# Start addresses of the weight rings in SBUF: from multiples of 2048 to 448 modulo 512

## The reference

```
def first_block(x, mem, ...):
    x = x + 0.5 * swiglu(rms_norm(x, norm_ffn1_w), ffn1_w_in, ffn1_w_out)      # d_ff 2816
    x = x + hybrid_mixer(rms_norm(x, norm_mix_w), w_in_mix, ...)               # SSD scan | differential attention
    x = x + memory_cross_attention(rms_norm(x, ..), rms_norm(mem, ..), w_cq, w_ck, w_cv, w_co)
    x = x + 0.5 * swiglu(rms_norm(x, norm_ffn2_w), ffn2_w_in, ffn2_w_out)
    return rms_norm(x, norm_final_w)

def second_block(x, p, ...):
    q, k, v, cb, cc, cu, ga, gc = split(rms_norm_2(x, g_pre_mix) @ w_in)
    o = stick_breaking_attention(q, k, v)
    y_conv = (cb * causal_depthwise_conv(cc * cu, w_conv)) @ w_conv_out
    x = x + rms_norm_2((gate_attn * (o @ w_attn_out) + gate_conv * y_conv) @ w_o, g_post_mix)
    x = x + rms_norm_2(square(relu(rms_norm_2(x, g_pre_mlp) @ w_up)) @ w_down, g_post_mlp)
    x = x + sigmoid(rms_norm_2(x, g_ple) @ w_ple_gate) * (p @ w_ple_proj)
```

## Time and profile before

| what | value |
|---|---|
| median of 3 runs | 2135.91 us (2134.52 to 2137.22) |
| span of the profiled execution | 2133.4 us |
| PE busy | 2114.8 us, 99% of the span, 10122 matmuls |
| POOL, DVE, ACT busy | 1120.5, 829.8, 803.6 us |
| granted TensorE clock | 1.00 |
| transfers | 207.71 MB, mean 97 GB/s |

### The profile page before, as it was taken

One profiled execution on the slowest core, in us unless ns is written; L12 is line 12 of the kernel. 1 busy time (PEld: TensorE's weight loads), 2 busy tenths in 40 slices (PEclk: granted clock), 3 DMA queues, 4 the chain that ended last, 5 costly groups with the idle time before them and its releaser, 6 DMA issues.

```text
span 2133.4 us, 29164 instructions
## 1 busy us (share of the span) xinstructions
PE 2114.8 (99%) x10122; PEld 1740.7 (82%) x10122; DVE 829.8 (39%) x1489; ACT 803.6 (38%) x1345; POOL 1120.5 (53%) x1493
## 2 busy tenths in 40 slices
PE   9999999999999999999999999999999999999999
PEld 7888888878887778877888888887787888888887
DVE  5222211762841766143322222208744474023244
ACT  5222232325834655323322223326554343122233
POOL 6555555673354337725655555554545466555554
PEclk9999999999999999999999999999999999999999
DMA  6322233233322213412332223321222223332322
GB/s 214 119 98 98 99 106 106 85 99 96 114 99 79 75 55 122 155 40 89 99 98 98 95 94 117 99 96 63 79 89 79 89 80 108 99 99 99 99 89 80
DMA packets 61344, 207.71 MB, mean 97 GB/s; under 512 B 6616, under 2 KB 8088, under 8 KB 61256
## 3 DMA queue, kind: packets, MB, share of 16 engines
q1 hardware_dynamic: 55216, 195.84, 27.8%
q10 hardware_dynamic: 6040, 10.65, 1.5%
HBM read 204.31 MB, written 4.77 MB: 98 GB/s over the span
## 4 chain that ended last, share of the span: by engine, by line
PE 42%; issue 28%; POOL 27%; DVE 2%; POOLq 0%; ACT 0%; DMA 0%; SPq 0%; DVEq 0%; ACTq 0%
POOL w_lo L463 27%; PE bank L516 11%; PE bank L518 11%; PE bank L517 11%; PE bank L678 1%; PE bank L680 1%; PE bank L679 1%; PE bank L908 1%; PE bank L932 1%; PE bank L840 1%; PE bank L920 0%; DVE gx_lo L2394 0%; DVE bank L2403 0%; PE bank L846 0%; DVE x L2405 0%
## 5 line engine op out<-in xcount | busy, mean ns | idle before, releaser
L463 POOL TENSOR_TENSOR w_lo<-w_raw,w_hi 128x256 fp32r<-128x256 f32 x1448 | 1087.1, 783 | 933.4 <-ACT w_hi L1283 933.3
L516 PE MATMUL bank<-gx_hi,w_hi 128*128 128x512 f32 (+1 forms) x1768 | 674.9, 382 | 7.8 <-DVE gx_lo L2394 4.5
L518 PE MATMUL bank<-gx_hi,w_lo 128*128 128x512 f32 (+1 forms) x1768 | 668.1, 378 | 0.0
L517 PE MATMUL bank<-gx_lo,w_hi 128*128 128x512 f32 (+1 forms) x1768 | 667.6, 378 | 0.0
L1283 ACT CAST w_hi<-w_raw 128x1024 fp32r<-128x1024 f32 x364 | 378.4, 1045 | 347.9 <-PE bank L518 291.8
L516 PEld LDWEIGHTS bank<-gx_hi,w_hi 128*128 128x128 f32 x1768 | 332.6, 188 | 74.2 <-DVE gx_lo L2394 6.4
L518 PEld LDWEIGHTS bank<-gx_hi,w_lo 128*128 128x128 f32 x1768 | 332.5, 188 | 62.1
L517 PEld LDWEIGHTS bank<-gx_lo,w_hi 128*128 128x128 f32 x1768 | 332.7, 188 | 60.5 <-issue 0.2
L516 PE MATMUL bank<-ff_hi,w_hi 128*128 128x512 f32 x352 | 136.9, 389 | 0.0
L517 PE MATMUL bank<-ff_lo,w_hi 128*128 128x512 f32 x352 | 136.9, 389 | 0.0
L518 PE MATMUL bank<-ff_hi,w_lo 128*128 128x512 f32 x352 | 136.9, 389 | 0.0
(11 more groups left out here) (358 smaller groups left out, 2703.4 us busy)
## 6 DMA issues: line engine op xcount, KB each, us to landing
w_raw<-wstream SPq DMA_DIRECT2D x364, 512.0 KB, 3.5
bias_spread<-bias_rows ACTq DMA_DIRECT2D x1, 2560.0 KB
square<-cum_rows ACTq DMA_DIRECT2D x8, 256.0 KB, 3.5
rfin_row<-cum_rows ACTq DMA_DIRECT2D x8, 256.0 KB, 3.1
outT<-ple_o SPq DMA_DIRECT2D x8, 256.0 KB, 2.0
x<-xT SPq DMA_DIRECT2D x3, 512.0 KB, 8.0
square<-bias_spread ACTq DMA_DIRECT2D x4, 256.0 KB, 2.6
rfin_row<-bias_spread ACTq DMA_DIRECT2D x4, 256.0 KB, 2.7
```

The lines of the kernel that those rows point to most:

```text
L463: ins = nc.gpsimd.tensor_tensor(w_lo[:, s, part], w_raw[:, s, part], w_hi[:, s, part].bitcast(F32), ALU.subtract)
L516: nc.tensor.matmul(dst, hi, rhs[0], start=first, stop=False)
L517: nc.tensor.matmul(dst, hi, rhs[1], start=False, stop=False)
L518: return nc.tensor.matmul(dst, lo, rhs[0], start=False, stop=last)
```

## The change

Ahead of the rings the cursor moves on by 448 bytes, and the order of the three is now `w_hi`, `w_lo`, `w_raw`. All three are 16 KiB long, so each begins at 448 modulo 512, and so does every block of 128 weights in them. `flip`, which nothing reads, is dropped from `consts` with its 128 columns; the slices of `consts` behind it shift by one. What lies from `rows` to `xrec` starts 64 bytes lower than before. REGION is at the same address as before, and with it every activation in it; `x`, `cols`, `wdt` and `gx` are ahead of the inserted bytes and stay as well. No engine's instructions are changed in kind, number, shape or order.

```diff
@@ -34,6 +34,7 @@
 LINE = 2048
+STATIONARY = 64
 RING = 4
@@ -162,10 +163,11 @@
         gx_hi = fixed("gx_hi", [DC, S], F32R)
         gx_lo = fixed("gx_lo", [DC, S], F32R)
-        w_raw = fixed("w_raw", [RING, UNIT])
+        cursor[0] += 512 - STATIONARY
         w_hi = fixed("w_hi", [RING, UNIT], F32R)
         w_lo = fixed("w_lo", [RING, UNIT], F32R)
-        consts = fixed("consts", [7 * P])
+        w_raw = fixed("w_raw", [RING, UNIT])
+        consts = fixed("consts", [6 * P])
         rows = fixed("rows", [NROWS])
@@ -195,7 +197,7 @@
-        ident, tri_le, ones, flip, neg_ge, neg_ones, tri_lt = (consts[:, i * P:(i + 1) * P] for i in range(7))
+        ident, tri_le, ones, neg_ge, neg_ones, tri_lt = (consts[:, i * P:(i + 1) * P] for i in range(6))
@@ -1610,7 +1612,7 @@
-            nc.scalar.copy(stick_r[:, 0:2, :], consts[:, 4 * P:6 * P].rearrange("p (a b) -> p a b", a=2))\
+            nc.scalar.copy(stick_r[:, 0:2, :], consts[:, 3 * P:5 * P].rearrange("p (a b) -> p a b", a=2))\
@@ -2543,7 +2545,7 @@
-    m = [np.eye(P, dtype=f), (i[:, None] <= i[None, :]).astype(f), np.ones((P, P), f), np.eye(P, dtype=f)[::-1],
+    m = [np.eye(P, dtype=f), (i[:, None] <= i[None, :]).astype(f), np.ones((P, P), f),
```

## The result

The kernel after takes 2151.47 us (median of 4 runs, 2150.16 to 2152.01) where the kernel before takes 2135.22 beside it: the ratio is 1.0075 with a 95% interval of 1.0061 to 1.0089. It is slower by 0.75%, where I had forecast 1.4% faster. The time is inside the stated range, but on its slow side, which I had given to the rivals, and outside the forecast's own range of 2086 to 2125 us.

A forecast was written before the change was run, and what follows sets the result against it. PE was taken as the bound, matmul count times pitch (start-to-start distance, 226.6 ns at 512 columns). Terms −31.9, −1.6 and +3.2 us net −30.3, off the median 2135.91: 2106 us, with 2078 to 2186 for 8 in 10.

The forecast's parts named there:

- The first term: 7344 matmuls of 512 columns with ring slices stationary: 4.35 ns less each, −31.9 us, ends −15.4 and −48.5.
- Ring slices as stationary, 512 columns: The step behind the first term: middle of 2.1 and 6.6 ns taken as gain on each of 7344 matmuls.
- the pitch of 220 to 224.5 ns: Sign that the forecast is right: start distance of 512-column matmuls in a window such as 1100 to 1122 us.
- 64 above costs, 64 below gains: Reading of two stages: stationary 64 bytes above moving costs 6.6 ns (`cv`), 64 below gains 2.1 ns (`ck`).
- Halves: 768 matmuls of 256 columns, `gx` and `up` in halves: 2.1 ns less each, −1.6 us.
- Token stages: 480 matmuls of `z`, `v`, `v2`, activations stationary and ring moving: 6.6 ns more each, +3.2 us.
- ACT, POOL, the transfers and the small tensors: Ring readers and writers off PE, and small tensors moved by 64 bytes: zero, being covered by PE's work.
- `ck` and `cv` at 128 apart: 192 and 96 matmuls whose operands come to 128 bytes apart: taken as 0, bounds ±0.4 and ±0.6 us.
- Rival 1: Plain 512-column matmuls lose a rhythm that needs equal starts: about +4.7 ns each, 2171 us; chance 0.22.
- Rival 2: Any stationary off a multiple of 512 costs what `cv` costs: +6.6 ns on 7344 matmuls, 2187 us; chance 0.14.
- Rival 3: Nothing happens: the pitch doesn't depend on where the ring stands, 2136 us; chance 0.10.
- Rival 4: Remainder beyond the columns goes almost entirely in the plain form: −11.6 ns on 7344 matmuls, 2052 us; chance 0.08.

The follow-up runs named there:

- rings0: Changed kernel with the three rings back on a multiple of 512, the 448 bytes behind them; 2135.49 us, ratio 1.0000 to the kernel before.
- all448: Changed kernel with `gx` and REGION also at 448 modulo 512, so operands start alike again; 2135.52 us, ratio 1.0003 to the kernel before.
- lo448: Changed kernel with `w_hi` on a multiple of 512 again, only `w_lo` and `w_raw` at 448; 2162.87 us, ratio 1.0127 to the kernel before.
- rings64: Changed kernel with its rings at 64 modulo 512 instead of 448; 2176.14 us, ratio 1.0190 to the kernel before.
- halves64: Changed kernel with rings at 0 modulo 256 and only the 16 units of 256-column matmuls 64 bytes higher; 2134.74 us, ratio 0.9999 to the kernel before.

## Why the prediction was wrong

**The first term had the wrong sign.** The step that failed is "Ring slices as stationary, 512 columns": I took −4.35 ns, the middle between 2.1 ns "of the right sign but half the columns" and 6.6 ns "of the right columns but the other sign". The sign came from `ck` at 256 columns, the size from `cv` at 512. Measured, the plain form went from 226.7 to 228.9 ns at its settled places, and on average over all its pitches without a pause from 227.05 to 229.08: a loss of 2.0 ns and not a gain of 4.35. In the trace the term is +14.4 us, where I had put −31.9. Of the signs named ahead, the pitch of 220 to 224.5 ns failed; the halves near 117.8, the token stages near 233 and the unchanged waits and engines all came.

**Why the sign did not carry over.** "64 above costs, 64 below gains" is wrong twice. At 512 columns the table has no gain on either side of 0: all distances cost but 16. At 256 columns the lowest pitch, 113.3, stands at +64, the side that "costs". What `ck` had over the earlier trace rows was not a gain of its distance over a neutral 0; at 256 columns 0 is a poor place, with 120.0. Equal starts are the best place for the one length and a poor one for the other, so a row of the one says nothing of the sign of the other. A pitch with all columns counted (213.3) was never near: the lowest at 512 columns in any trace was 226.7.

**The small terms held.** Halves: −1.6 us forecast, −0.9 in the trace, with 120.0 to 117.8 ns. Token stages: +3.2 us forecast, +2.5 in the trace, with 233.3 ns at their settled place as expected. ACT, POOL, the transfers and the small tensors: 0 forecast, and the runs bound them at about 0.1% either way, `rings0` the small tensors and `consts`, `all448` the engines and transfers that use the rings. The `ck` and `cv` at 128 apart: taken as 0, measured +0.8 and −1.0 ns, under 0.2 us each. One bound was too low: with the far end of 6.6 ns PE's share of a unit would fall by 24 × 6.6 = 158 ns, not by 0.1 us at most; nothing hangs on it.

**Why 14.4 and not 16.** At the settled places the loss is 2.2 ns, and 7344 × 2.2 would be 16.2 us. The rest is at the breaks: the first ten pitches behind one, 101 times in each trace, average 230.0 ns before and 230.2 after. There before is hardly better than after, so the change costs next to nothing. A single stretch misleads here: behind one break after has 233.3 (901.28 us above) where before has 231.3, and behind the next one it is the other way round, 229.7 against the 230.8 of the earlier trace rows:

```profile
912.63 0.39 PE L519 MATMUL bank<-gx_lo,w_hi 128*128 128x512 f32 x1
...
914.93 0.39 PE L520 MATMUL bank<-gx_hi,w_lo 128*128 128x512 f32 x1
```

**The rivals.** Rival 1 (the rhythm is lost) described the pattern rightly: a favourable step that holds only while both operands start alike, and an unfavourable one at 256 columns. `all448` has both back with equal starts, at another address. It was wrong on what comes in its place: not a pitch that wanders between 224 and 236 ns at a mean of +4.7, but new steady patterns, at +2.2 mostly and +6.6 in places. Its 2171 us is 20 too high. Its row, the 16-column weights at 231.7, mixes slices at 0, 64, 128 and so on; `lo448` shows one mixture, of 0 and 192, that is dearer than its parts, so such a row was no safe price for a ring that starts alike everywhere. Rival 2 is excluded by `all448`. Rival 3 is excluded by the result, and its argument for was sound for multiples of 512 (the period is 256). Rival 4 had no run near it.

**The rule against the rows.** The Trainium skill (TensorE: Matmul & The Clock Gate, Step-by-step: what each phase is for) has the moving operand and the next weights read through independent ports, so that loading takes no read bandwidth from the running matmul. What I had drawn from it, that no address of a weight can move the pitch, the runs contradict: with nothing moved but the rings the whole kernel goes from ratio 1.0000 (`rings0`) to 1.0075 (after) and 1.0190 (`rings64`). Following the rows against the rule was right; reading a direction out of two of them wasn't.

**What stays open.** No run shows which part of the chip makes the remainder of 13.3 ns and its patterns. That stationary and moving reads disturb each other, and lock into a rhythm, fits the dependence on their distance, the dependence on neighbouring loads, and the jump at a break; but this is argued, not shown. Nor do I know what picks the pattern after a break.

## What to carry to other kernels

Where PE is busy throughout, read the pitch from start times, by form and at several places, before you count matmuls: up to 1.9% of the time hung on a start address, and neither the waits nor PE's share of the span (99% in both) shows it. Start stationary and moving operands at the same address modulo 256 bytes for long fp32r matmuls of 512 columns, and don't mix; of the distances tried none was better at that length, and a ring at 192 cost 0.75% of this kernel, one at 64 cost 1.9%. A difference found at one matmul length is no evidence for another one, not even of its sign.

## What the runs showed that I had not expected

- One form with operands in the same places has more than one steady pitch: 228.9 and 233.3 ns at distance 192, 113.3 and 117.8 at distance 64 with 256 columns. In `halves64` it changed across four small matmuls.
- The dependence has a period of 256 bytes and steps of 16 matter: 16 costs nothing, 32 costs 6.7 ns, and 240 costs 0.9.
- In the trace of after, PE's granted clock falls for a moment near 1728 us of the span. What PE did ahead of it: 2.01 of 4 us busy.

```profile
1724.00:1728.00 4.00, 2.01 (x13) 1.74 (x13) 3.45 (x8) 2.17 (x4) 2.78 (x5) 0.95 0.57 194
1728.00:1732.00 4.00, 3.82 (x22) 3.62 (x20) 2.37 (x7) 1.54 (x5) 3.57 (x6) 0.62 0.32 109
```

The columns are span, busy us of PE, PEld, DVE, ACT and POOL, the granted clock, DMA share and GB/s. Matmuls of 256 columns there are 213 ns apart, which is the lower level of 1.2 GHz. The pauses of PE ahead of it are there in the trace of before too, without the fall. The change isn't needed for it: `rings0`, which has before's pitch and time, has it too and for longer. In the 4 us in which it begins PE is busy for 3.11:

```profile
1712.00:1716.00 4.00, 3.11 (x18) 2.90 (x19) 3.48 (x7) 2.57 (x5) 2.98 (x4) 0.78 0.41 131
1716.00:1720.00 4.00, 4.00 (x21) 4.00 (x20) 2.69 (x7) 1.54 (x5) 3.43 (x6) 0.50 0.40 131
```

And seven of the 19 runs of before beside `rings0` have a mean granted clock below 1.00 (0.998 or 0.999). In after the stretch is too short for more than about 1.7 us (4 us at 0.62 and 4 at 0.95); the 16 us are not from here.
